# Second attention's probabilities: turned in 32x32 blocks by VectorE and moved by SBUF to SBUF transfers, in place of turns by TensorE

## What is computed

```
s = q . k * HEAD_DIM ** -0.5 + bias            # query blocks of 128, the keys of this block and the one before
s = where(in band, s, -inf)
p = softmax(concat([s, sink]))[..., :-1]       # the sink takes part in the sum and is dropped
o = einsum('bnhgqs,bnshd->bnqhgd', p, v)       # the sum over keys: p is needed with the keys on the partitions
return o.reshape(B, S, N_HEADS * HEAD_DIM) @ w_out
```

## Time and profile before

| | us |
|---|---|
| median of the three runs (lowest, highest) | 2211.14 (2210.64, 2211.28) |
| span of the profiled execution, first to last instruction | 2209.0 |
| PE busy | 2197.2 |
| VectorE (DVE), ScalarE (ACT), GpSimd (POOL) busy | 1445.2, 1106.9, 550.7 |
| second attention, scores of block 0 to output of block 11 | 1265.3 to 1393.3 |

### The profile page before, as it was taken

The page is one execution under the profiler, slowest core; times in us unless marked ns, Lnnn a source line. Parts: engine busy times, 40 slices in busy tenths (PEclk is TensorE's granted clock), DMA queues, the critical chain, the costliest instruction groups (busy, mean ns, idle before and its releaser), DMA issues.

```text
span 2209.0 us, 34195 instructions
## 1 busy us (share of the span) xinstructions
PE 2197.2 (99%) x11625; PEld 1878.9 (85%) x11625; DVE 1445.2 (65%) x1925; ACT 1106.9 (50%) x1654; POOL 550.7 (25%) x531
## 2 busy tenths in 40 slices
PE   9999999999999999999999999999999999999998
PEld 7888988888888888888888887888888888888887
DVE  6877765555664565555566667567785688756875
ACT  6445555453453454445455455565553455534553
POOL 3202220350240141053000033005540245403431
PEclk9999999999999999999999999999999999999999
DMA  7675335556555555556555653545555555555554
GB/s 254 232 230 163 115 128 204 170 190 208 191 190 192 189 189 192 186 192 193 187 185 179 227 171 135 193 160 188 195 188 196 192 183 192 189 195 192 186 209 149
DMA packets 118072, 414.21 MB, mean 188 GB/s; under 512 B 12896, under 2 KB 18048, under 8 KB 117472
## 3 DMA queue, kind: packets, MB, share of 16 engines
q1 hardware_dynamic: 111600, 401.37, 53.9%
q10 hardware_dynamic: 6384, 11.70, 1.7%
HBM read 409.29 MB, written 2.15 MB: 186 GB/s over the span
## 4 chain that ended last, share of the span: by engine, by line
PE 98%; DVE 1%; ACT 1%; issue 0%; DMA 0%; DVEq 0%; ACTq 0%
PE bank L486 33%; PE bank L494 17%; PE bank L543 7%; PE bank L545 7%; PE bank L544 7%; PE bank L1059 4%; PE bank L1060 4%; PE bank L1061 4%; PE bank L599 1%; PE bank L601 1%; PE bank L600 1%; PE bank L619 1%; PE bank L994 1%; PE bank L656 1%; PE bank L796 1%; PE bank L798 1%
## 5 line engine op out<-in xcount | busy, mean ns | idle before, releaser
L1100 DVE TENSOR_TENSOR wboth<-raw,wboth 128x1024 fp32r<-128x1024 f32 x756 | 982.2, 1302 | 607.8 <-ACT wboth L1802 607.1
L1802 ACT CAST wboth<-raw 128x1024 fp32r<-128x1024 f32 x756 | 790.9, 1049 | 711.5 <-PE bank L545 241.6
L486 PE MATMUL bank<-A,wboth 128*128 128x512 f32 x2928 | 705.1, 391 | 0.3 <-DVE wboth L1100 0.3
L486 PEld LDWEIGHTS bank<-A,wboth 128*128 128x128 f32 x2928 | 537.0, 188 | 104.6 <-issue 1.0
L494 PEld LDWEIGHTS bank<-A,wboth 128*128 128x128 f32 x2928 | 376.7, 191 | 14.8
L494 PE MATMUL bank<-A,wboth 128*128 128x256 f32 x2928 | 384.0, 283 | 0.0
L543 PE MATMUL bank<-wboth,H 128*128 128x512 f32 x576 | 224.6, 390 | 0.0
L545 PE MATMUL bank<-wboth,H 128*128 128x512 f32 x576 | 224.2, 389 | 0.0
L544 PE MATMUL bank<-wboth,H 128*128 128x512 f32 x576 | 224.1, 389 | 0.0
L2257 POOL TENSOR_TENSOR bias<-z,rs 128x256 f32<-128x256 f32 x64 | 75.7, 1182 | 481.2 <-DVE z L1131 391.6
L2257 POOL TENSOR_TENSOR PT<-z,rs 128x256 f32<-128x256 f32 x88 | 73.4, 835 | 465.4 <-DVE z L1131 464.8
(11 more groups left out here) (293 smaller groups left out, 2409.1 us busy)
## 6 DMA issues: line engine op xcount, KB each, us to landing
raw<-wstream SPq DMA_DIRECT2D x756, 512.0 KB, 3.3
bias<-bias_rows ACTq DMA_DIRECT2D x6, 512.0 KB, 5.4
x<-xrows ACTq DMA_DIRECT2D x1, 2048.0 KB, 10.0
bias<-grows ACTq DMA_DIRECT2D x2, 1024.0 KB, 6.1
out<-x SPq DMA_DIRECT2D x8, 256.0 KB, 2.1
x<-xT SPq DMA_DIRECT2D x7, 256.0 KB, 4.6
pA<-bias_rows ACTq DMA_DIRECT2D x2, 512.0 KB, 8.9
Sm<-grows ACTq DMA_DIRECT2D x1, 1024.0 KB, 5.8
```

The source lines that it names most:

```text
L486: last = nc.tensor.matmul(bank(j)[:, :], whi[:, s, cols(i)], moving(j, k), start=(k == 0), stop=(k == K - 1))
L1100: V.tensor_tensor(wlo[:, s, :], raw[:, s, :], whi[:, s, :].bitcast(F32), ALU.subtract).then_inc(lo_ready, 1)
L1802: C.copy(whi[:, s, :], raw[:, s, :]).then_inc(hi_ready, 1)
```

## The change

- **Layout.** A block's slot of `Sm` now holds, for each query on a partition, runs of 32 keys with the heads between them, (run, head, 32), where it held (head, key).
- **Flip.** VectorE turns the whole slot in place, as 4x32 squares of 32x32 (`swa_flip`). Each square is then right in itself and on the wrong partitions.
- **Carry.** SP issues 16 transfers a block (`swa_carry`), one for each pair (i, j) of a band of 32 source partitions and one of 32 target partitions, 32 KB each, into one of two halves of `PT`: rows of two runs of 512 bytes for blocks of the second tile, one run of 1 KB for the others. They stand between the loads of weights: six before the load of piece f + 7, five before f + 8, five before f + 9, where f is the flip's place. The loads of these pieces are written out one by one, in place of the loop.
- **Waits.** SP waits for the flip and for the output two blocks earlier. PE's output and VectorE's maxima three blocks later wait for the landing of all 16.
- **Removed.** PE's turns and both copies from PSUM.
- **Places.** Outputs come four to five pieces later (14, 17, 19 for 10, 13, 15; in the last pair 37, 40, 42 for 34, 36, 37). The first 16 pieces of `wo2` have another order (`WO2_FIRST`), with those that read the last pair at its end. The scores, maxima, exponentials and reciprocals keep their places.

```diff
-SWA_AT = {"score": (5, 8, 10), "turn": (9, 12, 14), "out": (10, 13, 15), "max": (6, 9, 11), "exp": (6, 9, 11), "inv": (8, 11, 13),
-          "copy": (10, 13, 15), "hi": (None, 14, 16), "lo": (None, 15, 17)}
-SWA_AT_LAST = {"score": (29, 32, 33), "turn": (33, 35, 36), "out": (34, 36, 37), "max": (30, 33, 34), "exp": (30, 33, 34),
-               "inv": (32, 35, 35), "copy": (34, 36, 37), "hi": (None, 37, 38), "lo": (None, 37, 38)}
+SWA_AT = {"score": (5, 8, 10), "max": (6, 9, 11), "exp": (6, 9, 11), "inv": (8, 11, 13), "flip": (10, 13, 15), "out": (14, 17, 19),
+          "hi": (None, 18, 20), "lo": (None, 19, 21)}
+SWA_AT_LAST = {"score": (29, 32, 33), "max": (30, 33, 34), "exp": (30, 33, 34), "inv": (32, 35, 35), "flip": (34, 36, 38),
+               "out": (37, 40, 42), "hi": (None, 41, 43), "lo": (None, 41, 43)}
...
+WO2_FIRST = [(f, h) for hs in ((0, 1, 2, 3), (4, 5), (6, 7)) for f in range(2) for h in hs]
...
+LOADED = 7
+CARRY = [range(0, 6), range(6, 11), range(11, 16)]
 def due(at, last, step, i):
...
-            return n // 3, t, e0, e1, Sm[:, n % 3 * 8 * P:(n % 3 + 1) * 8 * P].rearrange("p (e k) -> p e k", e=e1 - e0)
+            return n // 3, t, e0, e1, swa_rows(n).rearrange("p (q e b) -> p e q b", e=e1 - e0, b=32)
+        def swa_rows(n):
+            return Sm[:, n % 3 * 8 * P:(n % 3 + 1) * 8 * P]
         def swa_score(t, e0, e):
...
-            with sp.Fori(1, NPIECE // SLOTS - 1) as it:
-                for j in range(SLOTS):
-                    load(it * SLOTS + (SLOTS + j), j)
-            for i in range(NPIECE // SLOTS * SLOTS, NPIECE):
+            def loads(a, b):
+                with sp.Fori(a // SLOTS, b // SLOTS) as it:
+                    for j in range(SLOTS):
+                        load(it * SLOTS + j, j)
+            def load_one(i):
...
+            def swa_carry(n, steps_of):
+                if 0 in steps_of:
+                    sp.wait_ge(swa["flipped"], n + 1)
+                    if n >= 2:
+                        sp.wait_ge(swa["o_done"], n - 1)
+                nk = SWA_BLOCKS[n % 3][0] + 1
+                src = swa_rows(n).rearrange("p (k j r) -> p j k r", k=nk, j=4)
+                dst = PT[:, n % 2, :, :].rearrange("p a b -> p (a b)").rearrange("p (i k r) -> p i k r", i=4, k=nk)
+                for step in steps_of:
+                    i, j = divmod(step, 4)
+                    sp.dma_start(dst[32 * j:32 * j + 32, i, :, :], src[32 * i:32 * i + 32, j, :, :]).then_inc(swa_landed[n % 3], 16)
+            first, last = PB["q2"] // SLOTS * SLOTS, (PB["q2"] + ATT_PIECES + LOADED) // SLOTS * SLOTS
+            loads(BLK, first)
+            for i in range(first, last):
+                for step, part in reversed([*enumerate(CARRY)]):
+                    for n in swa_due("flip", i - PB["q2"] - LOADED - step):
+                        swa_carry(n, part)
+                load_one(i)
+            loads(last, NPIECE // SLOTS * SLOTS)
+            for i in range(NPIECE // SLOTS * SLOTS, NPIECE):
+                load_one(i)
...
-            def swa_turn(n):
-                _, t, _, _, probs = swa_block(n)
-                pe.wait_ge(swa["scaled"], n + 1)
-                for b in range(2):
-                    if n:
-                        pe.wait_ge(swa["pt_dve" if b else "pt_act"], n)
-                    for i in range(4):
-                        src = probs[:, 4 * b + i, :] if t == 0 else probs[:, i, b * P:b * P + P]
-                        last = nc.tensor.transpose(psum[6 + b][:, i * P:i * P + P], src, ident)
-                    last.then_inc(swa["turned"], 1)
             def swa_output(n):
...
                     pe.wait_ge(swa["o_ready"], 2 * g)
-                pe.wait_ge(swa["pt_act"], n + 1)
+                pe.wait_ge(swa_landed[n % 3], 256 * (n // 3) + 256)
...
-                    if kt == t:
-                        pe.wait_ge(swa["pt_dve"], n + 1)
...
-                                                PT[:, kt, e0 + half:e1:2, :], start=(kt == 0), stop=(kt == t))
-                if n % 3:
-                    last.then_inc(swa["o_done"], 1)
+                                                swa_probs_of(n, kt, half), start=(kt == 0), stop=(kt == t))
+                last.then_inc(swa["o_done"], 1)
             def swa_after(i):
...
-                for n in swa_due("turn", i):
-                    swa_turn(n)
                 for n in swa_due("score", i):
...
-                    dve.wait_ge(swa["turned"], 2 * n - 4)
+                    dve.wait_ge(swa_landed[n % 3], 256 * (n // 3))
                 dve.wait_ge(swa["scores"], n + 1)
...
-                    V.tensor_tensor_reduce(probs[:, e - e0, :], swa_score(t, e0, e), swa_bias(g, e)[:, (1 - t) * P:], 1.0, -3e38,
+                    scores, near = (r.rearrange("p (q b) -> p q b", b=32) for r in (swa_score(t, e0, e), swa_bias(g, e)[:, (1 - t) * P:]))
+                    V.tensor_tensor_reduce(probs[:, e - e0, :, :], scores, near, 1.0, -3e38,
...
-            def swa_copy(n):
-                dve.wait_ge(swa["turned"], 2 * n + 2)
-                V.tensor_copy(swa_turned_to(n, 1), psum[7][:, :].rearrange("p (e q) -> p e q", e=4)).then_inc(swa["pt_dve"], 1)
+            def swa_flip(n):
+                dve.wait_ge(swa["scaled"], n + 1)
+                V.transpose(swa_rows(n), swa_rows(n)).then_inc(swa["flipped"], 1)
             def swa_lo(n):
...
-                    last = C.activation(probs[:, e - e0, :], probs[:, e - e0, :], ACT.Exp, bias=nmx[:, i:i + 1],
+                    last = C.activation(probs[:, e - e0, :, :], probs[:, e - e0, :, :], ACT.Exp, bias=nmx[:, i:i + 1],
...
-            def swa_copy(n):
-                act.wait_ge(swa["turned"], 2 * n + 1)
-                C.copy(swa_turned_to(n, 0), psum[6][:, :].rearrange("p (e q) -> p e q", e=4)).then_inc(swa["pt_act"], 1)
             def swa_hi(n):
...
-                act.wait_ge(swa["o_done"], 2 * g + 2 - t)
+                act.wait_ge(swa["o_done"], 3 * g + 3 - t)
...
-                for n in swa_due("copy", i):
-                    swa_copy(n)
...
-                if i == 38:
-                    act.wait_ge(swa["turned"], 2 * NBLOCK)
+                if i == 41:
+                    for n in (NBLOCK - 3, NBLOCK - 2):
+                        act.wait_ge(swa_landed[n % 3], 256 * (n // 3) + 256)
...
-                    if i == 32 + WO_FIRST.index((f, 7)) + 1:
+                    if i == 32 + WO2_FIRST.index((f, 7)) + 1:
...
-                G.tensor_tensor(probs, probs, coef[:, 8 * t + e0:8 * t + e1].unsqueeze(2).to_broadcast([P, e1 - e0, (t + 1) * P]),
-                                ALU.mult).then_inc(swa["scaled"], 1)
+                by = coef[:, 8 * t + e0:8 * t + e1].unsqueeze(2).unsqueeze(3).to_broadcast([P, e1 - e0, 4 * (t + 1), 32])
+                G.tensor_tensor(probs, probs, by, ALU.mult).then_inc(swa["scaled"], 1)
```

More of the change, by code:

```diff
@@ L334, in program @@
             "scores", "max", "step", "shift", "sinkdiff", "exp", "sinkexp", "inverse", "scaled",
-            "turned", "pt_act", "pt_dve", "o_done", "o_hi", "o_ready")}
+            "flipped", "o_done", "o_hi", "o_ready")}
+        swa_landed = [sem(f"swa_landed{i}") for i in range(3)]
         bias_in = [sem(f"bias_in{i}") for i in range(4)]
@@ L406, in swa_bias, with swa_probs_of @@
             return bias[:, m, e // 2, ::-1] if m < 3 else pAf[:, e // 2, ::-1]
-        def swa_turned_to(n, b):
-            t, e0, e1 = SWA_BLOCKS[n % 3]
-            return PT[:, 0, 4 * b:4 * b + 4, :] if t == 0 else PT[:, b, e0:e1, :]
+        def swa_probs_of(n, kt, half):
+            t = SWA_BLOCKS[n % 3][0]
+            runs = PT[:, n % 2, :, :].rearrange("p a b -> p (a b)").rearrange("p (i k e b) -> p k e i b", i=4, k=t + 1, b=32)
+            return runs[:, kt, half::2, :, :]
         def swa_out(buf, n, part):
@@ L999, in _ @@
             pe.wait_ge(z_ready, 4 + UB["wo2"])
-            for i, (f, h) in enumerate(WO_FIRST):
+            for i, (f, h) in enumerate(WO2_FIRST):
                 if (f, h) == (1, 0):
@@ L1630, in _ @@
             for i in range(ATT_PIECES + 2):
-                for n in swa_due("copy", i):
-                    swa_copy(n)
+                for n in swa_due("flip", i):
+                    swa_flip(n)
                 for n in swa_due("lo", i):
@@ L2123, in square @@
                 else:
-                    act.wait_ge(piece_used, SLOTS + PB["wo2"] + (WO_FIRST.index((f, 7)) + 1 if f < 2 else 8 * f + 8))
+                    act.wait_ge(piece_used, SLOTS + PB["wo2"] + (WO2_FIRST.index((f, 7)) + 1 if f < 2 else 8 * f + 8))
                 if f:
@@ L2408, with rows_out @@
     misc = np.concatenate([gates, a["nsa_cmp_w2_k"][0], a["nsa_cmp_w2_v"][0]], axis=1)
-    def rows_out(w):
+    def rows_out(w, order_of):
         by_piece = rows(w).reshape(4, BLK, BLK, P, P)
-        first, half = zip(*WO_FIRST)
+        first, half = zip(*order_of)
         return np.concatenate([by_piece[list(first), list(half)], by_piece[2:].reshape(-1, BLK, P, P)]).reshape(-1, P, P)
```

(4 more changed lines are left out.)

## The result

| | before | after |
|---|---|---|
| median (lowest to highest), 4 runs each on one chip | 2210.89 (2210.46 to 2211.28) | 2237.85 (2235.75 to 2240.13) |
| span of the profiled execution | 2209.0 | 2233.9 |
| mean granted clock of TensorE | 0.999 | 0.994 |

The ratio is 1.0121, with a 95% interval from 1.0109 to 1.0134: 1.2% slower, 27 us, where +8 were forecast. The measured 2237.85 lies above the forecast's range (2215 to 2226) and above the whole one (to 2229). In the profiled executions the difference is 24.9 us; that of after was the quickest of its four runs.

A forecast was written before the change was run, and what follows sets the result against it. PE was taken to bound the kernel: -9.8 us of its work, plus 18 us waiting because SP's queue needs 134 us where PE gives 116, made +8, 2219 us; own range 2215 to 2226, whole range 2204 to 2229.

The forecast's parts named there:

- The flip, 1.2 us: VectorE's block transpose of 128x1024, 1.2 us each and hidden; a rival said 2.5, some 4 us more.
- PE's own work, -9.8: On PE, 12 turns removed save 10.4 us, dearer successors of outputs add 0.6: -9.8 us.
- neighbourhoods: Wide matmuls after an output block on its own on PE cost about 0.12 us more; 5 x 0.12 = 0.6 added.
- Movement, 0.13 us a transfer and hidden: On the DMA engines, each 32 KB transfer takes 0.13 us, range 0.1 to 0.38, hidden beside other work.
- the rival of the DMA engines: At 0.38 us a transfer the DMA engines become the bound and weights come late: about 2230 us; chance 0.10.
- Landing, 2.1: The last transfer on SP's queue lands 2.1 us after its issue.
- SP's work, 130.2: SP's issues from first flip to last transfer: 128 x 0.63 + 64 x 0.56 + 30 loads x 0.46 = 130.2 us.
- The upper end: Top of the whole range, 2229 us: issues at 0.68, 192 of them at 0.05 more add 10.
- PE gives 116 us: From the first flip's end at 1281.0 to the last output at 1396.9, PE gives SP's queue 116 us.
- The slack of the loads: Weight loads behind SP's waits have 7 to 8 us of slack, more than the 6.9 of eleven transfers ahead.
- The one of 0.47 an issue: Every SP issue costs 0.47 us whatever it moves, only the last pair stays tight: -6, 2205 us; chance 0.27.
- The one in between: SP's issue price between the 0.47 rival and the forecast's mean of 0.59 to 0.65; chance 0.21.

The follow-up runs named there:

- run 1: The change with none of the 192 transfers; PE and VectorE wait for the flip instead, SP's waits go too: 2202.72 us, ratio 0.9964 to the kernel before.
- run 3: The change with all 16 transfers a block, each cut to half its bytes: 2236.06 us, ratio 1.0111 to the kernel before.
- run 6: The change with four of each block's sixteen transfers issued from ScalarE's queue, 12 left on SP: 2214.82 us, ratio 1.0016 to the kernel before.
- run 4: The change with the same transfers reading weights in DRAM instead of the probabilities in SBUF: 2228.17 us, ratio 1.0077 to the kernel before.
- run 2: The change with every second transfer left out, eight a block: 2202.72 us, ratio 0.9963 to the kernel before.
- run 7: The change with 8 transfers a block issued by SP, 4 by ScalarE, and four diagonal tiles copied by ScalarE: 2205.02 us, ratio 0.9973 to the kernel before.
- run 5: The change with each block's four diagonal tiles copied by ScalarE, so SP issues 12: 2211.16 us, ratio 1.0006 to the kernel before.
- run 9: The change with eight wrong-data transfers a block in four forms (within SBUF or from DRAM, one or two runs), to price issues: 2202.71 us, one run.
- run 8: The change with each block sent out to DRAM in one or two transfers and back in four: 2209.22 us, ratio 0.9989 to the kernel before.

## Why the prediction was right in its direction and wrong in its size

- **The flip, 1.2 us: right.** A row of after:

```profile
L1633 DVE STREAM_TRANSPOSE Sm<-Sm x12: 1233/1236/1240, 1279.4 to 1404.0; 128x1024 f32<-128x1024 f32 x12
```

- **PE's own work, -9.8: 1.4 too much.** In run 1 busy time falls by 8.4 (2197.2 to 2188.8), and PE gets 0.7 of idle time more. The outputs' operand in runs of 32 numbers costs nothing, as taken: in run 1 the next matmuls start 1.01 us behind an output, as before. By subtraction 10.4 - 8.4 = 2.0 stand where I had 0.6 for neighbourhoods; no run takes this term, or the 10.4, by itself.
- **Movement, 0.13 us a transfer and hidden: right.** SP's queue went from 53.9% to 54.5% of 16 engines' span, which is some 27 us for 192, 0.14 each; against run 1, whose page has 54.4% without the transfers, it is 20 us, 0.10 each. Runs 3 and 6 show that it is hidden, and end the rival of the DMA engines.
- **Landing, 2.1: right.** The last transfer is issued at 1427.2, and the output that waits for it starts at 1429.18.
- **SP's work, 130.2: the step that failed.** I took 0.56 for a plain transfer, 0.63 for one in two runs, 0.46 for a load, each with the step to the next. Measured with it: 0.66 for both kinds (118.4 us by 192, and 0.045), 0.62 for a load (17.3 by 30, and 0.045). So 192 x 0.66 + 30 x 0.62 = 145.3 in place of 130.2: some 4 us from the transfers in two runs, 6.5 from the plain ones, 5 from the loads. Two causes. The sum "0.43 + 0.1 for within SBUF" mixes two prices that are not added, and the ACT rows of 0.47 to 0.54 that it leaned on were each the first after a wait; and I gave the loads behind transfers the price of loads behind loads, where run 4 shows that a load's issue goes by what is ahead of it. Besides, six of the 192 took over 0.9 us, 4.1 over the common price together. The means say 0.66; the medians, 0.64. The upper end had a slip too: 0.68 for all is 0.05 more for 128 transfers and 0.12 for 64, which adds 14 and not 10, and the loads had no range at all. With the 14, and the loads at 0.62, it is some 2238 in place of 2229.
- **PE gives 116 us: right.** In run 1 the last output starts at 1398.12, where 1396.9 was forecast. In after it starts at 1429.18, 31.1 later, in place of 18: PE's idle places up to there sum to 25.9 us for 1.6 in run 1, which is 24.3 of it, and the rest is work at the lower clock. By the forecast's own formula with the measured prices, 145.3 + 2.1 + 2 - 116 = 33.
- **The slack of the loads: right for PE.** PE waited for weights nowhere in the rows of after, though ScalarE did for seven loads (15.5 us). VectorE's maxima waited for landings nine times, 28.5 us, and PE once for a piece drained late because of it (2.21 us): told of as a possibility, and part of the 31.
- **The clock: not in the sum.** Behind PE's waits it fell. PE's busy time is 7.9 us longer than in run 1 (2196.7 for 2188.8), but most of it lies ahead of the last output, in time that SP set anyway, for it had gaps of 1.7 us only; I read this from the rows, no run takes the clock alone away. What lies behind the last output counts: its 1.98 for 1.08, and three wide matmuls from 1431.09 to 1432.53, where run 1 has 0.80 us. Together 1.5.

The sum of the spans is -7.7 + 31.1 + 1.5 = +24.9, which is what they differ by.

**The rivals.** The one of 0.47 an issue did not come true, for its price was wrong. What it says of a kernel whose SP is in time holds: where SP is relieved, the kernel is at 2202.7 (run 2) to 2205.0 (run 7), for its 2205. The one in between needs 114 to 125 us of SP's work, which the change doesn't have; run 5, with 113.6, is at its 2211. The one of the DMA engines had the number nearest to the measured one (2230), by luck: what it says of bytes and packets, runs 3 and 6 refute. The flip took 1.24 us, not 2.5.

The estimate of 0.43 us for every kind, from 512 cycles of "DMA: Bandwidth & Descriptors" in the Trainium skill, agrees with the issues from DRAM in one run a row (0.43), and not with the 0.59 of the others. The remark on that page of the Trainium skill, in "Issuing engines are not separate DMA queues", that the sequencer's time is usually small beside the transfer, doesn't hold for the movement of 32 KB here: 0.59 beside 0.10 to 0.14. From issue to landing it is 2.3 us, but landings overlap and a queue's issues don't. The same section of the Trainium skill says that a second issuing engine saves only sequencer time; runs 6 and 7 agree, and here that time was the loss.

## What to carry to other kernels

Before giving a queue many small transfers, add up its issues over the stage, 0.6 us and more for each within SBUF, those of the loads in between at the same rate, and set the sum against the time of the busiest engine. Here, against 116 us, eight issues a block (82 us by the same prices) were free, twelve (114) cost 8 us, and with sixteen (145) the overhang was paid in full. Fewer transfers help where smaller ones don't. If it doesn't fit, use a second issuer, or copy what stays on its partitions. Put the reserve where the last block waits, for there it is used up first.

## What the runs showed of the hardware

- An issue on SP takes 0.33 us behind a wait (a load). Behind another it takes 0.43 from DRAM where the source or the target is one run a row (32 KB in run 9, 128 KB in run 8), 0.59 within SBUF or from DRAM in two runs on both sides, whatever the bytes (16 to 64 KB), and 0.51 out to DRAM (run 8). Some three in a hundred take 0.9 to 1.9.
- A load's issue takes 0.58 behind transfers of the 0.59 kind and 0.42 behind those of the 0.43 kind (run 4).
- On ScalarE's queue an issue within SBUF takes 0.62. ScalarE finishes beside it what stands ahead, and starts what stands behind 0.10 us or more after the last issue (run 6).
- VectorE turns 128x1024 numbers in squares of 32x32 in 1.236 us, in place, nearly the time of a subtraction of that size.
- PE's clock went to its 1.2 GHz level behind idle times of 2.30, 3.14, 4.65 and 6.48 us in after, 5.67 in run 6 and 2.65 in run 8, but not behind 2.20 in after or 3.43 in run 5 (granted 1.00 from 1395 to 1410 us, where run 6 had 0.80 from 1395 to 1412). In run 3 it went there behind 2.23 (0.79 from 1318 to 1326) and not behind 3.13 (1.00 from 1350 to 1370). The length of the wait alone doesn't decide it.
